# First feed forward: up and down slabs interleaved, 13 slabs by seven block products, two weight sums added by DMA

## The chip, the cores and the metric

The kernel runs on one core of a Trainium2 chip. The metric is the device time of one execution in microseconds (us), the median of several runs. TensorE does the matrix products into PSUM (eight banks of 512 float32 columns for each of 128 partitions), VectorE and ScalarE the elementwise work, Pool (GpSimd) small things and some DMA issues, SP the DMA issues of the weights. Each engine works through a queue of its own, in order; they meet by semaphores.

## The reference

Two transformer blocks on 256 tokens of width 1024, float32. The part that is changed is the feed forward of the first block:

```python
u = rmsnorm(h, norm_ff_g) @ w1          # (256, 1024) @ (1024, 4096)
h = h + jnp.square(jax.nn.relu(u)) @ w2 # (256, 4096) @ (4096, 1024)
```

Before it stand the mixer and a cross attention, behind it the second block (gated mixing of three branches and a convolutional feed forward). All of them stream weights in the same way.

## The kernel before

Weights stream through the core in slabs of 256 rows or columns, 128 x 2048 elements (1 MB) each, in the order that `plan` lists. A slab `n` is loaded by SP into one of three buffers (`raw`, slot `n % RING`), then split: ScalarE rounds it to `whi` (function `hi`, line 1389) and VectorE takes the rest, `wlo = raw - whi` (function `lo`, line 1944). A product in float32 accuracy is three matmuls (function `mm3`, lines 718 to 720): high by high, high by low, low by high. `whi` and `wlo` have three slots too, so slab `n + 3` is split when TensorE is done with slab `n` (`slab_done`), and slab `n + 3` is loaded when slab `n` is split (`lo_ready`). Each engine's program lists these steps by slab: at step `n`, ScalarE and VectorE do what comes after slab `n` and then split slab `n + 3`.

The feed forward has 16 up slabs (`w1`, called u0 to u15 here) and 16 down slabs (`w2`). An up slab gives 256 hidden columns in transposed form: `t_slab`, 16 products of 128 x 128 by 128 x 256, into one of three banks of `tb` in turn. ScalarE takes relu out of the bank into `ru` (line 1695), which frees it (`act_emptied`); VectorE squares into `sq` (line 2305), ScalarE copies the high part (`hid_hi`, line 1699), VectorE the low part (`hid_lo`, line 2319). All 16 up slabs come first, then the 16 down slabs, each adding its 256 hidden rows to four banks of `acc` (`row_slab`, 8 products of 128 x 128 by 128 x 512, for two tiles of tokens, two halves of columns and two blocks of rows).

Six of the down slabs (1, 3, 5, 7, 9, 11; list `SEVEN`) are done with seven products in place of eight, by Strassen's scheme in Winograd's form (`seven_slab`). A slab is four blocks B11, B12, B21, B22. Three products use blocks of the slab itself, four use sums of blocks (forms). VectorE makes four weight sums in place in `raw` (`forms`, lines 2331 to 2335), ScalarE copies their high parts (`forms_hi`, line 1717, into the room of `xhi`) and VectorE the low parts (`forms_lo`, line 2343). On the hidden side VectorE makes sums of the four 128-column blocks after the square (lines 2310 to 2313), with high and low parts in `sum_hi` and `sum_lo`. Four of the seven products collect in four banks of `tb` over the six slabs and are added to `h` by VectorE after slab 11 (`fold`, lines 2351 to 2361); the other three go straight into `acc`.

The last down slab (`last_row_slab`) goes by quarters: after each quarter VectorE adds it to `h` (`residual`, line 1984), and TensorE transposes the sum for the next stage (`turn`).

Of the kernel before, what the change touches and what calls it, by code (L numbers as in the profile page):

```python
# [16 lines left out]
F32 = mybir.dt.float32  # L17
# [7 lines left out]
P = 128  # L25
D = 1024
KT = D // P
T = 256
# [7 lines left out]
RING = 3  # L36
SLAB = 2048
# [6 lines left out]
PAD = 16  # L44


def plan(w):
# [40 lines left out]
    cols("w1", w["w1"], 0, 16)  # L88
    rows("w2", w["w2"], 16)
# [20 lines left out]
def two_blocks(nc, w, out):  # L110
# [14 lines left out]
    SEVEN = [first["w2"] + j for j in (1, 3, 5, 7, 9, 11)]  # L125

    landed = [0] * NS
    for n in range(NS):
        landed[n] = (landed[n - RING] if n >= RING else 0) + (16 if n < first["cv"] and n not in SEVEN else 32)

    with ExitStack() as ctx:
# [63 lines left out]
        with ExitStack() as r3:  # L195
            hid_hi = sb("hid_hi", [P, FF1 // P, T], F32R, at=r3)
            hid_lo = sb("hid_lo", [P, FF1 // P, T], F32R, at=r3)
            ru = sb("ru", [P, 512], at=r3)
            sq = sb("sq", [P, 512], at=r3)
            sum_hi = sb("sum_hi", [P, len(SEVEN), 3 * P], F32R, at=r3)  # L200
            sum_lo = sb("sum_lo", [P, len(SEVEN), 3 * P], F32R, at=r3)
# [55 lines left out]
        memT_in, mem2T_in, ml = sem("memT_in"), sem("mem2T_in"), sems("ml", "hi lo")  # L257
# [25 lines left out]
        sev = sems("sev", "t hi lo kept folded")  # L283
# [31 lines left out]
        lasts = [first["wo"] + 3, first["xo"] + 3, first["w2"] + 15, first["w3"] + 3, NS - 1]  # L315
# [3 lines left out]
        TURNED = {"h1": first["wo"] + 3, "h2": first["xo"] + 3, "x2": first["w2"] + 15}  # L319
# [116 lines left out]

        FORMS_HI, FORMS_LO = (room[:, 32:32 + SLAB].rearrange("p (s c) -> p s c", c=512) for room in (xhi_room, xlo_room))
        sums = xn[:, 0, 0:3 * P]

        def halves(t):  # L440

            return t[:, 0:4:3, :], t[:, 1:3, :]
# [11 lines left out]
        def _(sp):  # L454
            def load(n, src=None, wait=None):
# [59 lines left out]
            for n in range(RING + 1, first["w1"]):  # L515
# [5 lines left out]
            w1v = w["w1"].rearrange("(k p) c -> p k c", p=P)  # L521
            loop("w1", lambda i, u: w1v[:, :, bass.ds(i * 768 + u * 256, 256)], 5)
            load(first["w1"] + 15)
            for n in range(first["w2"], first["cv"]):
                load(n)
# [7 lines left out]
        def _(pool):  # L533
# [115 lines left out]
            pool.dma_start(turned_mem, w["mem2T"]).then_inc(mem2T_in, 16)  # L649
# [4 lines left out]
            for m in range(1, LEVELS):  # L654
# [8 lines left out]
            scale_cross()  # L663
            square_scale()
# [50 lines left out]
        def _(pe):  # L715
# [17 lines left out]
            def t_slab(n, hi, lo, bank, value=None, fresh=None):  # L733
# [4 lines left out]
                for c in range(slabs[n][3] // P):  # L738
                    o = tb[:, bank + c // 2, (c % 2) * T:(c % 2) * T + T]
# [35 lines left out]
            def seven_slab(j, hi, lo):  # L775

                n = first["w2"] + j
                i, k = SEVEN.index(n), 2 * j
                b_hi, b_lo = slab(whi, n, 2).rearrange("p k (s c) -> p (k s) c", c=512), \
                    low_slab(n, 2).rearrange("p k (s c) -> p (k s) c", c=512)  # L780
                first_one, last_one = i == 0, i == len(SEVEN) - 1

                def whole(kt, t):
                    return hi[:, kt, t * P:t * P + P], lo[:, kt, t * P:t * P + P]

                def summed(a):
                    return sum_hi[:, i, a * P:a * P + P], sum_lo[:, i, a * P:a * P + P]

                split_ready(n)
                mm3(tb[:, 0, :], *whole(k, 0), b_hi[:, 1, :], b_lo[:, 1, :], first_one, last_one)  # L790
                mm3(acc[:, 0, 0, :], *whole(k + 1, 0), b_hi[:, 2, :], b_lo[:, 2, :], False, False)
                mm3(acc[:, 1, 0, :], *summed(2), b_hi[:, 3, :], b_lo[:, 3, :], False, False)
                pe.wait_ge(sev["lo"], 2 * i + 1)
                mm3(tb[:, 1, :], *summed(0), FORMS_HI[:, 0, :], FORMS_LO[:, 0, :], first_one, last_one)
                mm3(tb[:, 3, :], *whole(k, 1), FORMS_HI[:, 3, :], FORMS_LO[:, 3, :], first_one, last_one)
                pe.wait_ge(sev["lo"], 2 * i + 2)
                mm3(tb[:, 2, :], *summed(1), FORMS_HI[:, 1, :], FORMS_LO[:, 1, :], first_one, last_one)
                mm3(acc[:, 0, 1, :], *whole(k + 1, 1), FORMS_HI[:, 2, :], FORMS_LO[:, 2, :], False, False)\
                    .then_inc(slab_done, 1)
# [396 lines left out]
            n0 = first["w1"] + 1  # L1196
            with pe.Fori(0, 5) as i:
                for u in range(RING):
                    pe.wait_ge(act_emptied, i * RING + (act_evacs[n0 + u] - RING))
                    t_slab(n0 + u, XHI["h2"], XLO["h2"], (u + 1) % RING, i * RING + (n0 + u + 1))  # L1200

            for j in range(15):
                pe.wait_ge(ffn["lo"], j + 1)
                if j == 1:
                    emptied(first["w1"] + 15)
                if first["w2"] + j in SEVEN:
# [1499 lines left out]
```

## Time and profile before

| | us |
|---|---|
| median of 3 runs | 884.2 (884.06 to 884.23) |
| the profiled execution | 884.08 |
| its span, first to last instruction | 882.2 |
| TensorE busy | 874.6 (99%) |
| VectorE busy | 647.6 (73%) |
| ScalarE busy | 502.4 (57%) |
| Pool busy | 117.9 (13%) |
| moved by DMA | 160.67 MB, 182 GB/s over the span |

The span is what the rows of the trace cover; the rest of an execution's time (1.9 us) lies around it. A row of a matmul gives its length in a pipeline, so consecutive matmuls overlap in the rows; the pace of a slab is read from the starts. "Idle before" tells how long an engine had stood still before an instruction and which other instruction released it.

### The profile page before, as it was taken

The numbers are of one execution on the slowest core, as the hardware profiler recorded it, in microseconds if no ns is written. First come the engines' busy times: TensorE is split into PE (matmuls) and PEld (weight loads), VectorE is DVE, ScalarE is ACT, GpSimd is POOL, SyncE is SP. The second block draws the span as 40 slices with busy tenths as digits, with TensorE's granted clock in tenths as the row PEclk, the third lists the DMA queues.
The fourth block names the chain that finished last, engine by engine and source line by source line (L and its number), as shares of the span: only waits on it lengthen the run. The fifth ranks groups of instructions, "written<-read, shape, count | busy, mean of one in ns | idle before, by whom it ended". The sixth has DMA issues, their size and how long they took to land.

```text
span 882.2 us, 15673 instructions
## 1 busy us (share of the span) xinstructions
PE 874.6 (99%) x6269; PEld 809.7 (92%) x6269; DVE 647.6 (73%) x881; ACT 502.4 (57%) x741; POOL 117.9 (13%) x136
## 2 busy tenths in 40 slices
PE   9999999999999999999999999999999999999997
PEld 9998988989989999888899989999998899999886
DVE  5887987656538887998775548978686788888643
ACT  7786655546547555545473356656634766666432
POOL 5561433000001000000142250001000100000000
PEclk9999999999999999999999999999999999999999
DMA  9969444354535666466556554354556386676641
GB/s 304 319 226 311 164 144 144 104 177 148 172 94 187 195 195 197 160 230 219 191 184 210 191 191 141 104 188 138 174 191 191 105 225 195 194 198 201 192 143 48
DMA packets 137399, 160.67 MB, mean 182 GB/s; under 512 B 4161, under 2 KB 113857, under 8 KB 137089
## 3 DMA queue, kind: packets, MB, share of 16 engines
q1 hardware_dynamic: 135280, 152.83, 54.1%
q0 software_dynamic: 1344, 6.03, 2.0%
q10 hardware_dynamic: 720, 1.06, 0.3%
q8 instruction: 38, 0.62, 0.3%
q14 instruction: 17, 0.13, 0.1%
HBM read 158.86 MB, written 1.05 MB: 181 GB/s over the span
## 4 chain that ended last, share of the span: by engine, by line
PE 98%; issue 1%; ACT 0%; DVE 0%; POOL 0%; DVEq 0%; POOLq 0%; ACTq 0%
PE tb L718 18%; PE tb L719 18%; PE tb L720 18%; PE acc L718 11%; PE acc L720 11%; PE acc L719 11%; PE acc L1043 1%; PE tb L1242 0%; PE tb L1122 0%; PE acc L1272 0%; PE tb L1140 0%; PE acc L1140 0%; PE acc L1290 0%; PE acc L1122 0%; PE tb L1241 0%
## 5 line engine op out<-in xcount | busy, mean ns | idle before, releaser
L1944 DVE TENSOR_TENSOR wlo<-raw,whi 128x2048 fp32r<-128x2048 f32 (+1 forms) x138 | 313.9, 2279 | 118.5 <-ACT whi L1389 117.9
L1389 ACT ACTIVATE whi<-raw 128x2048 fp32r<-128x2048 f32 (+1 forms) x138 | 261.4, 1896 | 140.6 <-PE acc L720 85.2
L718 PE MATMUL tb<-xhi,whi 128*128 128x256 f32 x1192 | 331.8, 278 | 0.2
L719 PE MATMUL tb<-xlo,whi 128*128 128x256 f32 x1192 | 329.5, 276 | 0.0
L720 PE MATMUL tb<-xhi,wlo 128*128 128x256 f32 x1192 | 329.5, 276 | 0.0
L718 PEld LDWEIGHTS tb<-xhi,whi 128*128 128x128 f32 x1192 | 224.1, 188 | 1.1 <-issue 1.0
L719 PEld LDWEIGHTS tb<-xlo,whi 128*128 128x128 f32 x1192 | 224.2, 188 | 0.1
L720 PEld LDWEIGHTS tb<-xhi,wlo 128*128 128x128 f32 x1192 | 224.0, 188 | 0.0
L720 PE MATMUL acc<-whi,xlo 128*128 128x512 f32 x112 | 44.0, 393 | 0.0
L718 PE MATMUL acc<-whi,xhi 128*128 128x512 f32 x112 | 43.8, 392 | 0.0
L719 PE MATMUL acc<-wlo,xhi 128*128 128x512 f32 x112 | 43.8, 391 | 0.0
L1893 ACT ACTIVATE cy<-tb,cols 128x256 f32<-128x256 f32 x44 | 22.5, 561 | 32.3 <-PE tb L720 32.3
L711 POOL TENSOR_TENSOR rs<-rs,half_neg 128x1 f32<-128x1 f32 x6 | 3.3, 553 | 266.8 <-DVE rs L2563 266.8
L719 PE MATMUL acc<-wlo,vhi 128*128 128x512 f32 x88 | 34.2, 389 | 0.0
L718 PE MATMUL acc<-whi,vhi 128*128 128x512 f32 x88 | 34.2, 389 | 0.0
L720 PE MATMUL acc<-whi,vlo 128*128 128x512 f32 x88 | 34.2, 389 | 0.0
L718 PE MATMUL acc<-whi,hid_hi 128*128 128x512 f32 x86 | 33.6, 391 | 0.0
L720 PE MATMUL acc<-whi,hid_lo 128*128 128x512 f32 x86 | 33.5, 389 | 0.0
L719 PE MATMUL acc<-wlo,hid_hi 128*128 128x512 f32 x86 | 33.5, 389 | 0.0
L2619 DVE SCALAR_TENSOR_TENSOR cy<-tb,cols,cy 128x255 f32<-128x255 f32 x44 | 19.2, 478 | 14.1 <-ACT cy L1893 14.1
L718 PE MATMUL tb<-mhi,whi 128*128 128x256 f32 x96 | 27.1, 282 | 0.0
L720 PE MATMUL tb<-mhi,wlo 128*128 128x256 f32 x96 | 26.6, 277 | 0.0
(448 smaller groups left out, 1598.2 us busy)
## 6 DMA issues: line engine op xcount, KB each, us to landing
raw<-in_w_in SPq DMA_DIRECT2D x37, 1024.0 KB, 5.2
raw<-in_w SPq DMA_DIRECT2D x26, 1024.0 KB, 5.4
raw<-in_w_up SPq DMA_DIRECT2D x44, 512.0 KB, 5.0
raw<-in_w_down SPq DMA_DIRECT2D x22, 512.0 KB, 4.2
raw<-in_w_xkv SPq DMA_DIRECT2D x8, 1024.0 KB, 5.3
raw<-in_w_out SPq DMA_DIRECT2D x8, 1024.0 KB, 4.9
raw<-in_w SPq DMA_DIRECT2D x12, 512.0 KB, 4.5
raw<-in_w_mem_kv SPq DMA_DIRECT2D x4, 1024.0 KB, 5.2
```

Of the source, the lines that this page charges most:

```text
L711: pool.tensor_tensor(r, r, half_neg[:, 0:1], ALU.pow).then_inc(tail_rs, 1)
L718: pe.matmul(o, a_hi, b_hi, start=start, stop=False)
L719: pe.matmul(o, a_hi, b_lo, start=False, stop=False)
L720: return pe.matmul(o, a_lo, b_hi, start=False, stop=stop)
L1043: last = pe.matmul(acc[:, 1, t, i * 64:i * 64 + 64], a[:, s], lvl_view(b[:, s], m)[:, :, 1, :], start=True, stop=True)
L1389: act.activation(whi[:, n % RING, cut], raw[:, n % RING, cut], ACT.Copy).then_inc(hi_ready, 1)
L1893: last = act.activation(cy[:, b, g, :], tb[:, b, g * T:g * T + T], ACT.Identity, scale=cols[:, bass.ds(j + a, 1)], bias=cols[:, bass.ds(j ...
L1944: dve.tensor_tensor(low(n)[:, cut], raw[:, n % RING, cut], whi[:, n % RING, cut].bitcast(F32), ALU.subtract).then_inc(lo_ready, 1)
L2619: last = dve.scalar_tensor_tensor(cy[:, b, g, 1:], tb[:, b, g * T:g * T + T - 1], cols[:, bass.ds(j + c, 1)], cy[:, b, g, 1:], ALU.mult, A ...
```

## The change

The up and down slabs of the first feed forward are no longer done in two runs but interleaved, in the order of `FIRST_FFN` (u an up slab, s a down slab by seven products, n a plain one). 13 of the 16 down slabs go by seven products; 3, 7 and 11 stay plain. A down slab needs the hidden rows of its own up slab only.

- PSUM: the seven products use four banks of `tb` and three of `acc`. The eighth bank, `acc[:, 1, 1, :]`, takes all up slabs but u0. TensorE starts an up slab when ScalarE has done relu and square of the one before.
- Weight sums: the scheme's signs are set so that T1 = B11 + B12, T3 = B12 + B22, T2 = T1 + B22, T4 = T2 + B21. SP loads B12 and B22 into a new tile `pairs` (two buffers) beside B11, B21 and B22 in `raw`; then Pool issues a DMA that adds B11 and B12 to them on the way (`add_blocks`). VectorE makes T2 and T4 (`weight_sums`). The forms have rooms of their own with two buffers (`forms_hi`, `forms_lo`).
- Hidden side: ScalarE squares too; VectorE makes four sums of 128 columns (`hidden_sums`); the seven blocks are split together (896 columns).
- The fold comes after s15, with n7 and n11 behind it, from a copy of the four `tb` banks that ScalarE makes in `pairs`.
- TensorE's loop over w1 and SP's are unrolled. Two semaphores of the transposed memories become one.

```diff
+FIRST_FFN = "u0 u1 u2 s0 u3 s1 u4 s2 u5 u6 s4 u7 s5 u8 s6 u9 u10 s8 u11 s9 u12 s10 u13 u14 s12 u15 s13 n3 s14 s15 n7 n11"
...
                 if n in SEVEN:
                     forms = raw_forms(n)
-                    for c, slots in enumerate((slice(1, 3), slice(0, 4, 3))):
-                        sp.dma_start(forms[:, slots, :], ap[:, :, c * 512:c * 512 + 512]).then_inc(raw_landed[n % RING], 16)
+                    i = SEVEN.index(n)
+                    sp.dma_start(forms[:, 1:3, :], ap[:, :, 0:512]).then_inc(raw_landed[n % RING], 16)
+                    sp.dma_start(forms[:, 3, :], ap[:, 1, 512:1024]).then_inc(raw_landed[n % RING], 16)
+                    if i >= 2:
+                        sp.wait_ge(sev["lo"], 2 * i - 3)
+                    sp.dma_start(pairs[:, i % 2, :, :], ap[:, :, 512:1024]).then_inc(raw_landed[n % RING], 16)
...
+            def add_blocks(n):
+
+                i = SEVEN.index(n)
+                pool.wait_ge(raw_landed[n % RING], landed[n])
+                if i >= 2:
+                    pool.wait_ge(sev["lo"], 2 * i - 3)
+                pool.dma_start(pairs[:, i % 2, :, :], slabs[n][1][:, 0, :].rearrange("p (a c) -> p a c", a=2),
+                               accum_op=ALU.add).then_inc(sev[f"acc{i % 2}"], 16)
+
+            add_blocks(SEVEN[0])
             square_scale()
 
             pool.dma_start(xn[:, 1, :], w["final_norm_g"].rearrange("(a c) -> a c", a=1).broadcast_to([P, D])
                            ).then_inc(gfin_in, 16)
+            for n in SEVEN[1:]:
+                add_blocks(n)
             gain_fin()
...
-            n0 = first["w1"] + 1
-            with pe.Fori(0, 5) as i:
-                for u in range(RING):
-                    pe.wait_ge(act_emptied, i * RING + (act_evacs[n0 + u] - RING))
-                    t_slab(n0 + u, XHI["h2"], XLO["h2"], (u + 1) % RING, i * RING + (n0 + u + 1))
-
-            for j in range(15):
+            for kind, j in ORDER[1:-1]:
+                if kind == "u":
+                    emptied(UP[j - 1] if j > 1 else first["xo"] + 3)
+                    t_slab(UP[j], XHI["h2"], XLO["h2"], None, whole=acc[:, 1, 1, :])
+                    continue
                 pe.wait_ge(ffn["lo"], j + 1)
...
-            pe.wait_ge(sev["folded"], 1)
-            last_row_slab("x2", hid_hi, hid_lo, 30)
+            j = PLAIN[-1]
+            pe.wait_ge(sev["kept"], 1)
+            last_row_slab("x2", plain_hidden(hid_hi, j), plain_hidden(hid_lo, j), 0)
...
+            def relu_square(j):
+
+                act.wait_ge(slab_done, UP[j] + 1)
+                if j:
+                    act.wait_ge(act_emptied, act_evacs[UP[j - 1]])
+                    act.activation(ru[:, :], acc[:, 1, 1, :], ACT.Relu).then_inc(act_link, 1)
...
+                act.wait_ge(act_link, count[0])
+                act.wait_ge(ffn["lo"], j)
+                act.activation(sq[:, 0:512], ru[:, :], ACT.Square).then_inc(act_emptied, 1)
...
+            for n, (kind, j) in enumerate(ORDER[:-1], first["w1"]):
+                if kind == "u":
+                    relu_square(j)
+                hi(n + RING)
+                if kind == "u":
+                    hidden_hi(j)
+                if n + RING in SEVEN:
+                    form_hi(n + RING, 0)
+                    form_hi(n + RING, 1)
+                if n == SEVEN[-1]:
+                    act.wait_ge(slab_done, n + 1)
+                    act.activation(pairs[:, :, :, :].rearrange("p i s c -> p (i s) c"), tb[:, :, :], ACT.Copy)\
+                        .then_inc(sev["kept"], 1)
...
+            def hidden_sums(j):
+
+                a11, a21, a12, a22, s1, s2, s4 = (sq[:, s * P:s * P + P] for s in range(7))
+                dve.wait_ge(act_emptied, act_evacs[UP[j]])
+                link(dve.tensor_tensor(s1, a22, a21, ALU.subtract))
+                dve.tensor_tensor(a21, a11, a21, ALU.subtract)
+                link(dve.tensor_tensor(s2, s1, a11, ALU.add))
+                dve.tensor_tensor(s4, a12, s2, ALU.subtract).then_inc(ffn["sq"], 1)
...
+            def weight_sums(n):
+
                 i = SEVEN.index(n)
...
+                dve.wait_ge(sev[f"acc{i % 2}"], 16 * (i // 2) + 16)
+                dve.wait_ge(lo_ready, n + 1)
+                link(dve.tensor_tensor(t2, t1, b22, ALU.add))
+                dve.tensor_tensor(b21, t2, b21, ALU.add).then_inc(sev["t"], 1)
...
+            for n, (kind, j) in enumerate(ORDER[:-2], first["w1"]):
+                if kind == "u" and seven(j):
+                    hidden_sums(j)
+                lo(n + RING)
+                if kind == "u":
+                    hidden_lo(j)
+                if n + RING in SEVEN:
+                    weight_sums(n + RING)
+                    form_lo(n + RING, 0)
+                    form_lo(n + RING, 1)
+                if n == SEVEN[-1]:
+                    fold()
```

`load` keeps its rule that the buffer of a seven-product slab is reloaded only when both of its forms are split (`if n - RING in SEVEN: sp.wait_ge(sev["lo"], ...)`). `form_hi` waits for the addition (first half) and for `weight_sums` (second half); `form_lo` follows it on VectorE.

## Rows read from the trace of the kernel before

**Rows 1.** The page's chain that ended last: shares of the span by engine.

```profile
PE 98%; issue 1%; ACT 0%; DVE 0%; POOL 0%; DVEq 0%; POOLq 0%; ACTq 0%
```

**Rows 2.** Busy us by stage, PEclk (granted clock), DMA share, GB/s.

```profile
272.00:446.00 174.00, 174.00 (x1170) 159.52 (x1169) 145.12 (x162) 99.77 (x110) 7.57 (x9) 1.00 0.60 196
```

**Rows 3.** Timeline of TensorE: start us, length us, line: first matmuls of slabs.

```profile
274.99 0.29 PE L718 MATMUL tb<-xhi,whi 128*128 128x256 f32 x1
...
356.66 0.39 PE L718 MATMUL acc<-whi,hid_hi 128*128 128x512 f32 x1
...
413.11 0.39 PE L718 MATMUL tb<-whi,hid_hi 128*128 128x512 f32 x1
...
417.87 0.39 PE L718 MATMUL acc<-whi,hid_hi 128*128 128x512 f32 x1
```

**Rows 4.** Waits from 270 to 446 us: total us, times, longest us.

```profile
ACT xhi L1717 <- DVE raw L2332: 17.6, 5, 4.0
```

**Rows 5.** Groups by line and shape, 272 to 441: busy us, mean ns, idle before.

```profile
L1944 DVE TENSOR_TENSOR wlo<-raw,whi 128x2048 fp32r<-128x2048 f32 x26 | 59.3, 2289 | 13.6 <-ACT whi L1389 13.5
L1389 ACT ACTIVATE whi<-raw 128x2048 fp32r<-128x2048 f32 x26 | 49.6, 1909 | 11.3 <-PE acc L720 11.3
...
L2343 DVE TENSOR_TENSOR xlo<-raw,xhi 128x1024 fp32r<-128x1024 f32 x12 | 14.5, 1221 | 0.0
L1717 ACT ACTIVATE xhi<-raw 128x1024 fp32r<-128x1024 f32 x12 | 12.7, 1062 | 19.6 <-DVE raw L2332 17.6 <-DVE raw L2335 2.0
...
L1944 DVE TENSOR_TENSOR wlo<-raw,whi 128x1536 fp32r<-128x1536 f32 x6 | 10.5, 1757 | 1.3 <-ACT whi L1389 1.2
...
L1695 ACT ACTIVATE ru<-tb 128x512 f32<-128x512 f32 x15 | 9.0, 601 | 30.9 <-PE tb L720 30.9
L1389 ACT ACTIVATE whi<-raw 128x1536 fp32r<-128x1536 f32 x6 | 8.9, 1488 | 3.8 <-PE acc L720 3.8
...
L2331 DVE TENSOR_TENSOR raw<-raw 128x512 f32<-128x512 f32 x6 | 4.2, 692 | 0.2
...
L2310 DVE TENSOR_TENSOR xn<-sq 128x128 f32<-128x128 f32 x6 | 1.8, 292 | 0.2
```

**Rows 6.** Timelines of ScalarE and of VectorE at the end of u0.

```profile
276.97 0.38 ACT L1707 ACTIVATE ru<-acc 128x256 f32<-128x256 f32 x1
...
277.38 0.69 DVE L2305 TENSOR_TENSOR sq<-ru 128x512 f32<-128x512 f32 x1 [0.40 <-ACT ru L1707]
```

**Rows 7.** DMA issues: count, KB each, us to landing; last: Pool's five into `xn`.

```profile
raw<-in_w SPq DMA_DIRECT2D x26, 1024.0 KB, 5.4
...
raw<-in_w SPq DMA_DIRECT2D x12, 512.0 KB, 4.5
...
gpost<-in_norm_ffn_post POOLq DMA_DIRECT2D x1, 512.0 KB, 4.0
...
DMA to landing us min/median/max: 5.4/7.0/7.8
```

**Rows 8.** Timeline of VectorE: first and last operation of the fold.

```profile
418.77 0.75 DVE L2351 SCALAR_TENSOR_TENSOR h<-ru,rs,h 128x512 f32<-128x512 f32 x1 [1.16 <-ACT ru L1731]
...
423.79 0.75 DVE L2351 SCALAR_TENSOR_TENSOR h<-ru,rs,h 128x512 f32<-128x512 f32 x1
```

**Rows 9.** TensorE's timeline at start and end; last: a stretch as in rows 2.

```profile
1.26 2.19 PE L906 MATMUL tb<-negF 128*128 128x128 f32 x9 [1.26 <-DVE negF L2008]
...
7.06 0.41 PE L720 MATMUL tb<-xhi,wlo 128*128 128x256 f32 x1
7.27 0.41 PE L718 MATMUL tb<-xhi,whi 128*128 128x256 f32 x1
...
7.84 0.28 PE L718 MATMUL acc<-xhi,whi 128*128 128x256 f32 x1
...
876.26 0.39 PE L720 MATMUL acc<-whi,vlo 128*128 128x512 f32 x1
...
881.50:882.20 0.70, 0.00 (x0) 0.00 (x0) 0.00 (x0) 0.00 (x0) 0.00 (x0) 0.53 0.00 0
```

More of the change, by code:

```diff
@@ L44, with ffn_order @@
 PAD = 16
+def ffn_order():
+    return [(step[0], int(step[1:])) for step in FIRST_FFN.split()]
 def plan(w):
@@ L87, in plan @@
     rows("xo", w["w_xo"], 4)
-    cols("w1", w["w1"], 0, 16)
-    rows("w2", w["w2"], 16)
+    first["w1"] = len(slabs)
+    for kind, j in ffn_order():
+        if kind == "u":
+            slabs.append(("T", w["w1"][:, j * 256:(j + 1) * 256].rearrange("(k p) c -> p k c", p=P), 8, 256, "act"))
+        else:
+            ap = w["w2"][j * 256:(j + 1) * 256, :].rearrange("(k p) c -> p k c", p=P)
+            slabs.append(("N", ap, 2, 1024, "dve" if len(slabs) == first["w1"] + 31 else None))
     wi = w["w_in_2"]
@@ L796, in seven_slab, with plain_slab @@
                 pe.wait_ge(sev["lo"], 2 * i + 2)
-                mm3(tb[:, 2, :], *summed(1), FORMS_HI[:, 1, :], FORMS_LO[:, 1, :], first_one, last_one)
-                mm3(acc[:, 0, 1, :], *whole(k + 1, 1), FORMS_HI[:, 2, :], FORMS_LO[:, 2, :], False, False)\
-                    .then_inc(slab_done, 1)
+                mm3(tb[:, 2, :], *part(S2), *form(T2), first_one, last_one)
+                mm3(acc[:, 0, 1, :], *part(A22), *form(T4), first_one, False).then_inc(slab_done, 1)
+            def plain_slab(j):
+                n, hi, lo = DOWN[j], plain_hidden(hid_hi, j), plain_hidden(hid_lo, j)
+                split_ready(n)
+                b_hi, b_lo = slab(whi, n, 2), low_slab(n, 2)
+                for t in range(TT):
+                    for c in range(2):
+                        for k in range(2):
+                            a, w = slice(t * P, t * P + P), slice(c * 512, c * 512 + 512)
+                            last = mm3(acc[:, c, t, :], hi[:, k, a], lo[:, k, a], b_hi[:, k, w], b_lo[:, k, w],
+                                       t * c == 1 and k == 0 and j == PLAIN[0], False)
+                last.then_inc(slab_done, 1)
@@ L1689, in _ @@
             sumsq("h2", h)
-            def relu_step(bank, done, j, dst):
-                act.wait_ge(slab_done, done)
-                act.activation(ru[:, :], tb[:, bank, :], ACT.Relu).then_inc(act_emptied, 1)
-            def relu_hi(j):
-                act.wait_ge(ffn["sq"], j + 1)
-                last = act.activation(hid_hi[:, 2 * j:2 * j + 2, :], sq[:, :], ACT.Copy)
-                if first["w2"] + j in SEVEN:
-                    last = act.activation(sum_hi[:, SEVEN.index(first["w2"] + j), :], sums, ACT.Copy)
-                last.then_inc(ffn["hi"], 1)
@@ new lines, in hidden_hi, with form_hi @@
+            def hidden_hi(j):
+                if seven(j):
+                    act.wait_ge(ffn["sq"], sum(seven(i) for i in range(j + 1)))
+                else:
+                    act.wait_ge(act_emptied, act_evacs[UP[j]])
+                cut = hidden_place(j)
+                act.activation(hid_hi[:, cut], sq[:, 0:cut.stop - cut.start], ACT.Copy).then_inc(ffn["hi"], 1)
+            def form_hi(n, half):
+                i = SEVEN.index(n)
+                if i >= 2:
+                    act.wait_ge(slab_done, SEVEN[i - 2] + 1)
+                if half == 0:
+                    act.wait_ge(sev[f"acc{i % 2}"], 16 * (i // 2) + 16)
+                else:
+                    act.wait_ge(sev["t"], i + 1)
+                src, cut = form_places(n, half)
+                act.activation(forms_hi[:, i % 2, cut, :], src, ACT.Copy).then_inc(sev["hi"], 1)
```

224 lines of the change are left out of this document (88 added, 136 removed).

## Prediction

> **What bounds the kernel now.** I read the chain that ended last first: 98% of it is TensorE [rows 1]. So time is won or lost here only where TensorE gets less work or waits. Then the table by stage, for the first feed forward [rows 2]: TensorE is busy for all of its 174 us, VectorE for 145 (83%), the DMA engines for 0.60 at 196 GB/s. So nothing is late there, but VectorE has only a sixth of its time to spare. Next the pace of a slab from the timeline. The first w1 slab ends at 274.99 and the first w2 slab starts at 356.66, with 15 w1 slabs between: 81.67 / 15 = 5.44 us each. A seven-product slab runs from 413.11 to 417.87: 4.76 us for 21 matmuls, 0.227 each [rows 3]; a plain one has 24 of them, 5.44. (The 0.39 us of a row is its pipelined length, not its pace.) Last the waits: ScalarE waited 17.6 us in five turns of up to 4.0 for the weight sums of VectorE, before it could copy them into forms [rows 4]. That costs nothing today, since nobody needs what is queued behind that copy soon. It is the row to keep in mind.
>
> **The gain.** Seven more slabs lose 3 of 24 matmuls: 7 x 3 x 0.227 = 4.8 us of TensorE. There is nothing else to win on the path: TensorE has no wait to remove.
>
> **What an up/seven pair costs off the path.** Durations are from [rows 5]; one for 896 columns lies between those for 512 and 1024. VectorE: wlo of an up slab 2.29, wlo of three quarters 1.76, four hidden sums 4 x 0.29, hid_lo 1.09, two weight sums 2 x 0.69, two form_lo 2 x 1.22: 10.1 us. ScalarE: 1.91 + 1.49 + two form copies 2 x 1.06 + relu 0.60 + square 0.60 + hid_hi 0.95 = 7.7. TensorE: 5.44 + 4.76 = 10.2. So in the alternating stretches VectorE is as loaded as TensorE and has no slack; the slabs that are split ahead cover it. The sums given to the DMA (2 x 0.69 for each seven slab) are what brings VectorE down to this. Unrolling the loop of w1 I cost at nothing: slabs outside loops have the same pace [rows 3]. The merged semaphore of the two transposed memories waits for the same transfers, so nothing there either; nor for Pool's steps that move behind the additions (the scale of h2, final_norm_g), which are first used at the fold and after it.
>
> **The new wait: one bank for all up slabs.** Before, u slabs went round three banks of tb. Now each but the first goes to the same half of acc, and TensorE may start one only when ScalarE has done relu and square of the one before. Where a seven slab stands between, its 4.76 us cover this. In four places two up slabs are neighbours (u1 u2, u5 u6, u9 u10, u13 u14) and nothing covers it. With ScalarE free it would be relu 0.60 + square 0.60 + hand-overs of some 0.5 = 1.7. (A hand-over is 0.03 at 277.35 to 277.38 [rows 6]; I estimate up to 0.1 each with the drain of a matmul, 0.39 long.) But ScalarE isn't free: its queue is in order, and ahead of that relu stand the two form copies for the slab three places on, the second of which waits for VectorE's weight sums, as in [rows 4], and now for a DMA as well.
>
> *u2.* Relu of u0 ends at 277.35 as now [rows 6]. Square and hand-over: 278.1. Four hidden sums to 279.4, beside ScalarE's copy of s0 (1.49) to 279.6. On VectorE wlo 1.76, hid_lo 1.09, two weight sums 1.4: 283.9. ScalarE: second form copy 1.06, relu and square of u1: 286.2. u1 ends at 274.99 + 5.44 = 280.4. TensorE waits 5.7 us.
>
> *u6, u10, u14* have the same neighbourhood. Let X be the end of u3 on TensorE (u7, u11). VectorE works on the forms of s2 then: relu, square 1.6, copy 1.5, wlo 1.76, hid_lo 0.69, sums 1.4, two form_lo 2.5: done at X + 9.6 with hand-overs. Only then may SP load s4, three places on, since `load` waits for both forms of the slab that held the buffer. The load is 1,280 KB in three DMAs; 512 KB took 4.5 and 1024 KB 5.4 [rows 7], so some 5.9. Then Pool issues the accumulating DMA, which lands after L. Then two sums 1.4, the form copy 1.06, relu and square of u5 1.2, hand-overs 0.5. Together X + 19.7 + L. TensorE ends u5 at X + 4.76 + 5.44 + 4.76 + 5.44 = X + 20.4. The wait is L - 0.7, and not under some 3: that is what copy, wlo, sums and form copy take after s2 has ended, if the addition is early.
>
> **L: no accumulating DMA is in the trace.** The nearest rows are Pool's plain ones: 4.0 for 512 KB in a quiet stretch, and 5.4 to 7.8 with a median of 7.0 for transfers of mostly 1024 KB [rows 7]. The addition brings 512 KB and reads as much of its target, so I take 7.0; low end 4.0, since it can't be quicker than the same transfer without an addition; high end 11, two such transfers in turn (7.0 + 4.0). The load on the DMA supports the upper half: a pair moves 1.05 + 1.31 + 0.52 = 2.88 MB in 10.2 us, 283 GB/s, against 196 at a share of 0.60 now [rows 2], which is a share of 0.87 before the price of adding. The wait is then 6.3 each, 18.9 for three (9.9 to 30.9). The Trainium skill (DMA: Bandwidth & Descriptors, Anatomy of one DMA) would give a plain Pool DMA of 512 KB some 3.2 us, an estimate from its fit of 2.0 us plus the bytes at 436 GB/s; the sum would then stand at the floor of 3 us for each wait. The rows of 4.0 and more say that it is longer here.
>
> **The end of the stage.** The fold's eight operations now follow s15, with two slabs behind them in place of four. In the trace they run from 418.77 to 424.54, 5.8 us [rows 8]. After the end of s15, at E: ScalarE splits a slab (1.9) and copies four banks (about 1.9), VectorE does wlo until E + 4.5, the fold until E + 10.3, and the first residual (0.75, as the fold's last row) until E + 11.1. TensorE has n7 (5.44) and two quarters of n11 (2.7) and needs the residual at E + 8.2. It waits 3.0 us (0 if VectorE gets to the fold 3 us earlier, 5 if ScalarE is late with the bank copy). For s15 and n7, whose splits come late behind the last addition, 0.5 (0 to 4).
>
> **The clock.** TensorE's last matmul starts at 876.26; the granted clock is 0.53 from 881.5 on, the half level (1.2 GHz) [rows 9]. At the start it works from 1.26, and at 7.06 matmuls of 256 columns are still 0.21 apart, twice the 0.113 of a w1 slab (5.44 / 48); the one at 7.84 has the length of a w1 row again (0.28, and 0.29 at 274.99). So four waits of 5.7 to 6.3 us can each drop the clock, and getting it back costs up to 6.5 us at half pace, 3.2 lost. I take 1.6 for each, 6.4 in all (0 to 13). The Trainium skill (TensorE: Matmul & The Clock Gate, HAM oscillation) says that a wait which lets the clock fall makes the next group of matmuls start slow, every time anew. By that rule the forecast holds; without it case B does.
>
> **Sum**, from the profiled execution: span 882.2 and 1.9 around it, 884.1, which is the median (884.2) within 0.1. -4.8 + 5.7 + 18.9 + 3.0 + 0.5 + 6.4 = +29.7: 913.8 us.
>
> **The rivals.**
> A (forecast): waits at the four neighbours as above, clock lost: 914, some 907 to 922. Chance 0.40.
> B: the same waits, the clock held: 884.1 + 23.3 = 907. For it: the half level shows only behind an idle stretch about as long as these waits [rows 9]. 0.25.
> C: the addition is quick (L = 4.0). Waits of 3.3, and the clock holds: -4.8 + 5.7 + 9.9 + 3.0 = +13.8, 898. For it: the 4.0 row; against it: the DMA's load. 0.13.
> D: the addition is slow and the DMA engines become the bound (L = 11): 30.9 in the three waits, 4 at s15 and n7: -4.8 + 5.7 + 30.9 + 3.0 + 4 + 6.4 = +45, 929. For it: a share of 0.87 before adding. 0.15.
> E (not slower): the bank is freed a slab earlier than I read. `emptied` compares with a running count of ScalarE's slabs; if that runs one ahead, a whole slab covers ScalarE's lateness, no u slab waits, and -4.8 + 3.0 gives 882.3. It decides from waits of under 1.8 us in all. Against it: one count is raised for each slab, and two writers of one bank need the wait. 0.07.
>
> **Numbers.** Runs of before lie within 0.2 us, and some 0.2% (1.8 us) can be told from no change. Range 897 to 930: it leaves out E, and what of D lies above and of C below. Faster 0.04, same 0.03 (both E), slower 0.93.
>
> **What would show it.** TensorE idle before the first matmul of u2, u6, u10 and u14, released by ScalarE's square, some 6 us each, and before the first turn behind n11, released by VectorE (3 us); no gap at other slabs. ScalarE idle before form copies, released by VectorE, and VectorE idle before its first weight sum of s4, s8, s12, for the DMA. Matmuls 0.45 us apart for some us after such a gap (A) or not (B). A landing of the additions near 4, 7 or 11 us tells C, A and D apart. Wrong would be: even gaps at all seven slabs (the DMA as a bound), or none at the up neighbours.

## The result and the profile after

The changed kernel takes 927.9 us (median of 4 runs, 925.98 to 929.01) against 884.1 beside it: a ratio of 1.0492 (1.0474 to 1.0511). It is 43.7 us slower. The forecast was 914 with a range of 897 to 930, so the time lies in the range, near its upper end. The profiled execution has a span of 926.1 us, 43.9 more than before; the accounts below are made from spans.

First the chain that ended last, shares of the span by engine (before: [rows 1]):

```profile
PE 79%; issue 8%; DMA 5%; DVE 5%; ACT 3%; POOL 0%; SPq 0%; POOLq 0%; DVEq 0%; ACTq 0%
```

A fifth of the chain is no longer TensorE. Next the stage's own stretch (busy us with counts of PE, PEld, DVE, ACT and POOL, then PEclk, DMA share, GB/s), which answers to [rows 2]:

```profile
272.00:490.00 218.00, 179.92 (x1152) 164.47 (x1152) 157.91 (x185) 122.67 (x135) 17.47 (x21) 0.91 0.69 201
```

TensorE stands for 38 of 218 us and its granted clock is 0.91 on average. No other engine is full: VectorE has 72%, the DMA engines 0.69. So something waits for something in turn, and the list of TensorE's waits (total us, times, longest) says where:

```profile
PE acc L763 <- ACT sq L1762: 34.2, 4, 9.8
PE tb L916 <- DVE h L2049: 3.8, 1, 3.8
PE acc L763 <- ACT pairs L1796: 0.2, 1, 0.2
```

Four waits for ScalarE's square and one for VectorE's residual. On TensorE's timeline they stand ahead of u2, u6, u10, u14 and the first turn, the five places of the prediction and, but for 0.2 us ahead of n7, no other. The second row of u6 belongs to the clock: it is 0.41 us long, where such a row has 0.28 at full pace:

```profile
286.21 0.58 PE L763 MATMUL acc<-xhi,whi 128*128 128x256 f32 x1 [5.25 <-ACT sq L1762]
...
334.51 0.58 PE L763 MATMUL acc<-xhi,whi 128*128 128x256 f32 x1 [9.50 <-ACT sq L1762]
334.89 0.41 PE L764 MATMUL acc<-xlo,whi 128*128 128x256 f32 x1
...
382.70 0.58 PE L763 MATMUL acc<-xhi,whi 128*128 128x256 f32 x1 [9.64 <-ACT sq L1762]
...
430.82 0.58 PE L763 MATMUL acc<-xhi,whi 128*128 128x256 f32 x1 [9.77 <-ACT sq L1762]
...
480.74 0.44 PE L916 MATMUL tb<-ident,h 128*128 128x128 f32 x2 [3.76 <-DVE h L2049]
```

What stands ahead of u6 is told by four timelines. X, the end of u3 and the start of s1, is at 304.35. SP:

```profile
313.53 0.37 SPq L498 DMA_DIRECT2D raw<-in_w  x1
313.94 1.21 SPq L499 DMA_DIRECT2D raw<-in_w  x1
315.19 0.44 SPq L502 DMA_DIRECT2D pairs<-in_w  x1
316.36 0.37 SPq L506 DMA_DIRECT2D raw<-in_w  x1
320.22 0.37 SPq L498 DMA_DIRECT2D raw<-in_w  x1
...
321.14 0.47 SPq L502 DMA_DIRECT2D pairs<-in_w  x1
```

Pool:

```profile
321.52 0.86 POOL L703 DMA_DIRECT2D pairs<-in_w  x1 [22.58 <-DMA pairs<-in_w]
```

VectorE:

```profile
330.74 0.69 DVE L2392 TENSOR_TENSOR raw<-pairs,raw 128x512 f32<-128x512 f32 x1 [6.12 <-DMA pairs<-in_w]
```

ScalarE:

```profile
330.80 1.06 ACT L1783 ACTIVATE forms_hi<-pairs 128x1024 fp32r<-128x1024 f32 x1 [8.04 <-DMA pairs<-in_w]
332.25 1.06 ACT L1783 ACTIVATE forms_hi<-raw 128x1024 fp32r<-128x1024 f32 x1 [0.40 <-DVE raw L2393]
333.21 0.58 ACT L1755 ACTIVATE ru<-acc 128x512 f32<-128x512 f32 x1
333.82 0.63 ACT L1762 ACTIVATE sq<-ru 128x512 f32<-128x512 f32 x1
```

SP issues the load of s4 at X + 9.2. It lands 8.0 us later (Pool's issue at 321.52 shows it), the addition another 9.2 us later, and form copies, relu and square take 3.8 to u6. TensorE had finished u5 at 324.84. From then to 333.21 the relu of u5, 1.2 us with the square, stood behind two copies for another slab. Beside the load of s4 SP issued that of u7 (316.36), and the three DMAs for s5 (320.22 to 321.14) just ahead of the addition. The 13 additions, from issue to landing:

```profile
DMA to landing us min/median/max: 5.4/5.7/9.2
```

Those of s4, s8 and s12 are the longest (9.2, 8.8 and 9.0); the one at 344.75, with no load just ahead, took 5.5. The DMA engines are 0.69 busy over the stage, but 0.89 during the addition of s4 (columns as above):

```profile
321.52:330.74 9.22, 3.49 (x31) 3.29 (x30) 1.76 (x2) 1.23 (x1) 0.86 (x1) 0.89 0.89 255
```

ScalarE's two kinds of wait before form copies answer to [rows 4], where VectorE's sums were the only one:

```profile
ACT forms_hi L1783 <- DMA pairs<-in_w: 26.7, 4, 8.0
...
ACT forms_hi L1783 <- DVE raw L2393: 23.8, 13, 2.5
```

Three long ones for additions and one of 3.1 us at s15, and 13 short ones for VectorE. Last the clock, in the wait for u6, in its first 4.5 us and after them (columns as above):

```profile
330.00:334.50 4.50, 0.00 (x0) 0.00 (x0) 3.68 (x5) 3.27 (x5) 0.86 (x1) 0.50 0.41 56
334.50:339.00 4.50, 4.49 (x21) 4.49 (x22) 3.77 (x7) 2.59 (x2) 0.00 (x0) 0.51 1.02 284
339.00:342.20 3.20, 3.20 (x30) 3.20 (x30) 0.58 (x1) 0.00 (x0) 0.00 (x0) 1.00 0.76 252
```

TensorE came out of the wait at the half level (1.2 GHz) and worked there for 4.5 us, then at the full one. The 48 matmuls of u2, u6, u10 and u14 took 7.9, 7.65, 7.45 and 7.3 us in place of 5.44.

The account of spans: -4.8 (seven products; a slab of them still takes 4.77, an up slab 5.47) + 34.2 (four waits) + 8.5 (slow matmuls, 2.46 + 2.21 + 2.01 + 1.86) + 3.8 + 0.2 = 41.9. Of the 2.0 us that are left, part is that idle time is counted from the end of a pipelined row and not from its pace; the rest I haven't assigned.

### The profile page after: what moved, and what is told of

Its sections match the earlier page's. It is cut to its first block, busy times and chain, and to the rows that moved or that the text cites. A ratio compares the mean times of both kernels' runs of the same rounds, so it can differ in the third digit from the quotient of the medians.

```text
span 926.1 us, 15681 instructions
## 1 busy us (share of the span) xinstructions
PE 880.2 (95%) x6248; PEld 814.3 (88%) x6248; DVE 659.2 (71%) x903; ACT 524.7 (57%) x765; POOL 123.5 (13%) x149
## 4 chain that ended last, share of the span: by engine, by line
PE 79%; issue 8%; DMA 5%; DVE 5%; ACT 3%; POOL 0%; SPq 0%; POOLq 0%; DVEq 0%; ACTq 0%
PE tb L763 14%; PE tb L765 14%; PE tb L764 14%; PE acc L763 10%; PE acc L765 9%; PE acc L764 9%; DMA pairs<-in_w 4%; PE acc L1103 1%; ACT whi L1447 1%; DVE wlo L2009 1%; DVE raw L2392 1%; DVE raw L2393 1%; DVE forms_lo L2400 1%; DVE hid_lo L2381 1%; DMA raw<-in_w_in 1%
## 5 line engine op out<-in xcount | busy, mean ns | idle before, releaser
L763 PE MATMUL tb<-xhi,whi 128*128 128x256 f32 x952 | 265.6, 279 | 0.3 <-issue 0.2
L764 PE MATMUL tb<-xlo,whi 128*128 128x256 f32 x952 | 263.2, 276 | 0.0
L765 PE MATMUL tb<-xhi,wlo 128*128 128x256 f32 x952 | 263.2, 276 | 0.0
L763 PEld LDWEIGHTS tb<-xhi,whi 128*128 128x128 f32 x952 | 179.0, 188 | 1.4 <-issue 1.2
L763 PE MATMUL acc<-xhi,whi 128*128 128x256 f32 x304 | 88.8, 292 | 34.2 <-ACT sq L1762 34.2
L763 PEld LDWEIGHTS acc<-xhi,whi 128*128 128x128 f32 x304 | 60.9, 200 | 35.3 <-ACT sq L1762 34.9
L764 PE MATMUL acc<-xlo,whi 128*128 128x256 f32 x304 | 87.7, 288 | 0.0
L765 PE MATMUL acc<-xhi,wlo 128*128 128x256 f32 x304 | 87.4, 288 | 0.0
L764 PEld LDWEIGHTS acc<-xlo,whi 128*128 128x128 f32 x304 | 61.0, 201 | 0.4
L765 PEld LDWEIGHTS acc<-xhi,wlo 128*128 128x128 f32 x304 | 60.7, 200 | 0.0
L763 PE MATMUL acc<-whi,xhi 128*128 128x512 f32 x112 | 43.9, 392 | 0.0
L764 PE MATMUL acc<-wlo,vhi 128*128 128x512 f32 x88 | 34.2, 389 | 0.0
L763 PE MATMUL acc<-whi,vhi 128*128 128x512 f32 x88 | 34.2, 389 | 0.0
```

Source lines behind the costliest of these rows:

```text
L763: pe.matmul(o, a_hi, b_hi, start=start, stop=False)
L764: pe.matmul(o, a_hi, b_lo, start=False, stop=False)
L765: return pe.matmul(o, a_lo, b_hi, start=False, stop=stop)
```

## The experiments

Theory Q is the prediction's: up slabs have one bank, ScalarE's queue is in order, and where two up slabs are neighbours the relu that frees the bank stands behind two form copies, which stand behind the addition. Its rivals: the bank and the copies take that time by themselves; the DMA queues set the pace; VectorE does; the slow matmuls aren't the clock. Each kernel was timed beside the kernel before; "above" means above that. "Slow" is what the 48 matmuls of a slab take over 5.44.

**e1: no addition.**

```diff
-                pool.dma_start(pairs[:, i % 2, :, :], ..., accum_op=ALU.add).then_inc(sev[f"acc{i % 2}"], 16)
+                pool.sem_inc(sev[f"acc{i % 2}"], 16)
```

> Edit: the Pool step that adds the two upper weight blocks in flight issues no DMA; it waits for the same load and then raises the same semaphore at once. T1 and T3, and with them T2 and T4, so lack one block each; everything else is computed. Theory Q (the relu that frees the one up bank stands in ScalarE's queue behind two form copies, which stand behind the addition's landing): the waits ahead of u6, u10 and u14 fall from 9.7 us to 2.8 to 3.8, the slow matmuls behind them (2.0 us each) go with them, u2's wait stays near 5.3 because there the copies and not the addition are late, the turn's wait stays: 14.5 to 17.5 us above the kernel before, 898.6 to 901.6 us. Rival B (the one bank and the copies in themselves are what takes the time, the addition lands beside them): the three waits lose 2 us at most, 920 us or more. Rival D (the queues are full and the loads set the pace; the addition is 10 of 171 MB): 925 us, with the waits on the loads instead.

911.6 us, a ratio of 1.0310 (1.0292 to 1.0328). TensorE's waits:

```profile
PE acc L762 <- ACT sq L1761: 16.6, 4, 5.3
PE tb L915 <- DVE h L2048: 3.3, 1, 3.3
```

u2 5.3 as before; u6, u10 and u14 3.9, 3.3 and 4.1, where Q had 2.8 to 3.8, so the addition is some 6 of each 9.7 us. But I had let the slow matmuls go with waits so short, and they stayed (2.2, 1.5, 3.0, 1.8, and 2.9 behind the turn). They are most of the 10 us by which I was off.

**e2: the relu ahead of the form copies.**

```diff
+                nxt = [ORDER[n + d - first["w1"]] for d in (1, 2) if n + d <= FFN_END]
+                ahead = n + RING in SEVEN and [k for k, _ in nxt] == ["u", "u"]
-                if kind == "u":
+                if kind == "u" and j not in early:
                     relu_square(j)
...
                 if kind == "u":
                     hidden_hi(j)
+                if ahead:
+                    relu_square(nxt[0][1])
+                    early.append(nxt[0][1])
                 if n + RING in SEVEN:
```

> Edit: where two up slabs follow each other, ScalarE does the relu and the square of the first of them ahead of the two form copies of the seven slab to come; nothing else moves and all is computed. Theory Q: the waits ahead of u6, u10 and u14 fall from 9.7 to about 1.8 us (relu, square and three handovers), u2's from 5.3 to about 2.5, none is followed by slow matmuls; but the additions still land as late, VectorE's sums and low parts come as late as before, and the slabs behind wait on VectorE instead (about 3.5 us ahead of u7, u11 and u15, some 1 us at others): about 23 us above the kernel before, 907 us. If VectorE had room to spare, only the turnaround stays: 10 us above, 894 us. Rival D (loads set the pace): 925 us or more, with the waits moved ahead of s4, s8 and s12.

910.9 us, 1.0314 (1.0283 to 1.0346), 4 us above what Q gave. The timeline has 2.31 us ahead of u2, 1.35 ahead of u6, u10 and u14, and 3.21, 2.40 and 2.21 ahead of u7, u11 and u15. Nothing but ScalarE's order was changed, and more than 8 us of each 9.7 are gone: it is the order that turns a late addition into this wait. Q had no slow matmuls; u2, u7 and u11 have them (1.6, 1.8 and 1.7 us), which is more than the 4 us. The waits behind are VectorE's, which still stands for the addition before it gets to the hidden sums of u5:

```profile
327.66 0.69 DVE L2399 TENSOR_TENSOR raw<-pairs,raw 128x512 f32<-128x512 f32 x1 [5.63 <-DMA pairs<-in_w]
```

**e3 and e5: the loads beside s4, s8 and s12 held back.** e3 holds the next load until the blocks of s4 are there and the one behind it until the addition is; e5 holds both until the addition is.

```diff
 # e3, in load(n); LONE holds s4, s8 and s12
+                for m in LONE:
+                    if n == m + 1:
+                        sp.wait_ge(raw_landed[m % RING], landed[m])
+                    elif n == m + 2:
+                        i = SEVEN.index(m)
+                        sp.wait_ge(sev[f"acc{i % 2}"], 16 * (i // 2) + 16)
 # e5, in load(n)
+                for m in LONE:
+                    if n == m + 1:
+                        i = SEVEN.index(m)
+                        sp.wait_ge(sev[f"acc{i % 2}"], 16 * (i // 2) + 16)
```

> Edit: SyncE issues the load of the slab after s4, s8 and s12 only when their own blocks have landed, and the load after that only when their addition has landed; nothing else moves and all is computed. Theory Q with the late landings put down to transfers issued beside them: the load of s4 lands 6 us after its issue instead of 7.9, the addition 5.5 us instead of 9.2, the waits ahead of u6, u10 and u14 fall from 9.7 to about 5, with half of the slow matmuls behind them: about 28 us above the kernel before, 912 us. Rival L (the addition takes 9 us there for another reason, its own two halves or the read of what it adds to): landings and waits stay, 928 us. Rival D (the queues are full): holding two loads back moves all that follows, above 930 us.

> Edit: the load of the slab after s4, s8 and s12 is issued only when the addition of that slab has landed (in e3 it went out just ahead of the addition, 320.4 and 320.6 us, so the addition still had 1 MB beside it); nothing else moves and all is computed. Theory Q with the late landing put down to the transfer beside it: the addition lands 5.4 to 5.7 us after its issue, as the ones without a load just ahead do, the waits ahead of u6, u10 and u14 are about 5 us instead of 9.7 (and 7.2 to 8.3 in e3), the clock still falls in them: 913 us. Rival L (the addition takes 8 to 9 us there whatever lies beside it): landings of 8 us and more, waits of 7 us or more, 921 us or more.

e3: 925.4 us, 1.0474 (1.0456 to 1.0491), not to be told from the changed kernel and 13 us above what Q gave. The edit put u7's 1 MB where s5's load had been, just ahead of the addition:

```profile
320.37 0.37 SPq L513 DMA_DIRECT2D raw<-in_w  x1
```

```profile
320.59 0.86 POOL L710 DMA_DIRECT2D pairs<-in_w  x1 [21.47 <-DMA pairs<-in_w]
```

Those are SP's and Pool's timelines; the landing of that one addition:

```profile
DMA to landing us min/median/max: 8.0/8.0/8.0
```

Those of s8 and s12 took 8.0 and 8.5. The waits were 7.2, 8.3 and 7.4 us. e5 has nothing beside the addition: 917.3 us, 1.0379 (1.0358 to 1.0400). The same addition:

```profile
DMA to landing us min/median/max: 5.5/5.5/5.5
```

The waits fell to 5.1, 5.1 and 4.6, as Q had them. So the long landing of these three comes from the load issued just ahead of them, and with none the DMA engines are 0.61 busy in place of 0.89:

```profile
321.23:326.73 5.50, 4.20 (x38) 4.00 (x36) 2.14 (x2) 1.23 (x1) 0.86 (x1) 1.00 0.61 95
```

The time fell 4 us less than expected, since slow matmuls stayed in full (2.8, 2.9, 1.6) and 1.7 more came behind the turn.

**e4: the waits filled.**

```diff
+                    if j in (6, 10, 14):
+                        pe.wait_ge(warm_ready, 2)
+                        for _ in range(82):
+                            pe.matmul(tb[:, 3, 0:T], negF[:, 0:P], XHI["h2"][:, 0, :], start=False, stop=False)
                     emptied(UP[j - 1] if j > 1 else first["xo"] + 3)
...
+            dve.memset(negF[:, :].bitcast(U32), 0).then_inc(warm_ready, 1)
```

> Edit: ahead of u6, u10 and u14 TensorE does 82 matmuls of 256 columns with a weight block of zeros into a bank that sums up (9.3 us at 0.113), then waits as before; the sums are unchanged by them. Theory K (the 2.0 us that each of these slabs takes above 5.44 are the clock, fallen in the wait): u6, u10 and u14 take 5.45 to 5.5 us instead of 7.3 to 7.65, the granted clock of the stretches 330:350, 370:390 and 430:450 is 0.95 or more, 6.0 us less than the changed kernel, 921.8 us. Rival (the slow start is the operands or the bank, not the clock): no less than 927 us, and matmuls of 0.21 us stay behind the wait.

919.8 us, 1.0410 (1.0388 to 1.0431): 8.1 less than the changed kernel with 246 matmuls more. The filled wait with the start of u6, and the rest of u6 with the first of s4 (columns as in the windows above):

```profile
324.00:334.50 10.50, 10.50 (x94) 10.41 (x93) 4.75 (x8) 4.68 (x5) 0.86 (x1) 1.00 0.79 178
334.50:339.00 4.50, 4.50 (x41) 4.46 (x40) 3.29 (x2) 1.35 (x3) 0.00 (x0) 1.00 0.83 268
```

The clock holds: TensorE does 41 matmuls in 4.5 us where it did 21, and u6, u10 and u14 take 5.4 to 5.5 us. So the slow matmuls are the clock; at the three slabs they had cost 6.1 us. Most of the other 2 us are fillings shorter than the waits (some 1.5 in all) and a quicker u2 (0.6).

**e6: e1 and e2 together.**

> Edits of e1 and e2 together (relu and square ahead of the form copies, and no addition issued, so that T1 to T4 lack a block each). In e2 the waits ahead of u7, u11 and u15 (3.2, 2.4, 2.2 us) are left. Theory Q (they too are the landing of the addition, for which VectorE's stream stands, with the hidden sums behind it): they go; left are 2.3 us ahead of u2, 1.4 us each ahead of u6, u10 and u14, 3.3 us ahead of the turn and the clock behind the first and the last of these: 8.6 us above the kernel before in the span, 892 us. Rival V (they are VectorE's own work, some 10.1 us of each pair's 10.24): waits of 2 us and more stay ahead of u7, u11 and u15, 900 us or more.

893.8 us, 1.0111 (1.0094 to 1.0128).

```profile
PE acc L762 <- ACT sq L1763: 6.4, 4, 2.3
PE tb L915 <- DVE h L2055: 3.8, 1, 3.8
```

The waits of e2 ahead of u7, u11 and u15 are gone, so they were the addition's too, reached through VectorE. Addition and order together explain 34 of the 44 us. What is left would not go with a free addition: an up slab behind another on one bank waits 1.35 us for relu, square and handovers.

**e7: VectorE makes the two sums.**

```diff
+                link(dve.tensor_tensor(pairs[:, i % 2, 1, :], pairs[:, i % 2, 1, :], pairs[:, i % 2, 0, :], ALU.add))
+                dve.tensor_tensor(pairs[:, i % 2, 0, :], pairs[:, i % 2, 0, :], raw_forms(n)[:, 1, :], ALU.add).then_inc(sev["acc0"], 1)
```

> Edit: no addition in flight; VectorE adds the two blocks itself, two more sums of 0.69 us for each seven slab, and ScalarE's form copy waits for these; nothing else moves and all is computed. Theory Q (what stands ahead of the relu decides, whoever makes it): the sums come after VectorE's low part of the same slab, so the copies wait nearly as long: 7 us ahead of u2 (5.3 before), 7 to 8 us ahead of u6, u10 and u14, 2 us more in the last slabs, and the clock behind each wait: 925 us. Rival A (only the landing of a transfer is the trouble, and VectorE has room): waits of 4 us as in e1, 911 us.

924.1 us, 1.0462 (1.0444 to 1.0479). Without any addition in flight:

```profile
PE acc L760 <- ACT sq L1759: 24.2, 4, 6.7
```

6.7 ahead of u2, 5.3 to 6.2 at the other three, where Q had 7 to 8, and 2.6 in the last slabs. So giving the sums to the DMA is not the mistake; what stands ahead of the relu is.

**e8: e2 and e5 together.**

> Edits of e2 and e5 together (relu and square ahead of the form copies, loads held until the addition has landed), all is computed. Theory Q: u2 waits 2.3 us, u6, u10 and u14 1.4 us each, VectorE is late by 1 to 1.5 us at some slabs behind them, the turn waits 3.8 us: 14 to 17 us above the kernel before, 899 us. Rival V (VectorE's work bounds the stage once the relu is free): no better than e2, 908 us or more.

915.5 us, 1.0350 (1.0326 to 1.0373), 5 us worse than e2. My forecast was 16 us off, and the rival's number came out, but not for its reason alone: ScalarE waits for additions at ten slabs (six in e2). I put that down to each load held back, which delays the next slab's addition.

```profile
ACT forms_hi L1790 <- DMA pairs<-in_w: 27.6, 10, 5.9
```

**e10: e2, and the addition's target loaded a slab earlier.**

```diff
                     sp.dma_start(dst, src).then_inc(raw_landed[n % RING], 16)
+                    load_pairs(n + 1)
...
-                pool.wait_ge(raw_landed[n % RING], landed[n])
...
+                pool.wait_ge((lam_in, bias_in)[i % 2], (64, 16)[i % 2] + 16 * (i // 2) + 16)
```

`load_pairs` loads B12 and B22 of the next slab, if that is a seven slab, on a semaphore of their own, for which alone Pool now waits.

> Edits of e2 (relu and square ahead of the form copies) and another: the blocks that the addition adds to are loaded one slab earlier, right behind the load before, so that the addition is issued and lands before the slab's other blocks; the order of the stage is that of the changed kernel, all is computed. Theory Q (once the addition lands before it is wanted it costs no more than none): the waits of e6 (2.3, 1.4 three times, 3.8 ahead of the turn), 893 to 896 us. Rival D (the additions' 7 MB slow the loads beside them wherever they stand): waits on slabs' loads, 903 us or more.

895.7 us, 1.0127 (1.0110 to 1.0144), with all additions made: 32 us less than the changed kernel and 1.9 above e6, which made none. An addition that lands before it is wanted costs next to nothing, whatever it does to the DMA engines.

**e9, e11: no up neighbours on one bank.** e9 leaves n0, n1 and n2 plain, so that u0 to u5 come first, in banks that are still idle, and up and seven slabs alternate from there. e11 adds the early addition of e10.

```diff
+FIRST_FFN = "u0 u1 u2 u3 u4 u5 s3 u6 s4 u7 s5 u8 s6 ... u14 s12 u15 s13 n0 s14 s15 n1 n2"
...
+            return {1: tb[:, 1, :], 2: tb[:, 2, :], 3: tb[:, 3, :], 4: acc[:, 0, 0, :]}.get(j, acc[:, 1, 1, :])
```

> Edit: the order of the stage. The three plain slabs become n0, n1 and n2 instead of n3, n7 and n11, so that the up slabs with no seven slab between them (u0 to u5) all stand at the beginning, where the seven accumulators are not yet in use: u1 to u4 go to four of those banks, u5 and all later ones to the one up bank as before, and from there on up and seven slabs alternate; the same 13 seven slabs and 13 additions, all is computed. Theory Q (what costs is two up slabs on one bank with form copies ahead of the relu, not the additions as such and not the seven products): no wait ahead of any up slab above 1.5 us, 3.8 us ahead of the turn with some 1.5 us of clock behind it, VectorE late by up to 0.3 us in each of ten pairs, 4.8 us gained by the seven products: 0.5 to 4.5 us above the kernel before, 884.5 to 888.5 us. Rival V (VectorE needs as much as TensorE in a pair and falls behind with no pause in 10 pairs): waits that grow from pair to pair, 895 us or more. Rival A (the additions cost wherever they stand): 900 us or more.

> Edits of e9 and the earlier addition of e10 together; all is computed. Theory Q: the additions are not late where up and seven slabs alternate, so landing them earlier changes nothing: within 1 us of e9. Rival A (the additions cost wherever they stand): 5 us or more less than e9. Rival D (they slow the loads): more than 1 us slower than e9.

e9: 904.3 us, 1.0226 (1.0209 to 1.0243). I was wrong by 16 us: the neighbours are gone, but now TensorE waits in the alternating stretch, for low parts of forms and weights that are late behind additions:

```profile
PE tb L766 <- DVE forms_lo L2408: 8.1, 6, 2.1
PE acc L766 <- DVE wlo L2017: 6.4, 6, 1.2
...
ACT forms_hi L1791 <- DMA pairs<-in_w: 27.3, 8, 5.4
```

In the changed kernel no addition was late there; the long waits at the neighbours had let all other queues catch up, and I had read their slack as belonging to the order. e11: 891.3 us, 1.0087 (1.0070 to 1.0104), 12.9 less than e9, where Q had no more than 1: rival A came out, by which the additions cost here too (e9's time fitted V as well). ScalarE waits once for an addition. What is left is 3.8 at the turn, 2.5 elsewhere, and pairs of 10.47 us (4.93 + 5.55) in place of 10.24.

**e12: the best version.** e11 with 12 seven slabs and four plain ones, so that three plain slabs follow s15, and with ScalarE's copy of the banks and VectorE's fold ahead of the next splits (also five idle banks for the first up slabs in place of four, and room for three hidden blocks in place of four):

```diff
-                hi(n + RING)
+                if n != SEVEN[-1]:
+                    hi(n + RING)
...
                         .then_inc(sev["kept"], 1)
+                    hi(n + RING)
...
-                lo(n + RING)
+                if n != SEVEN[-1]:
+                    lo(n + RING)
...
                     fold()
+                    lo(n + RING)
```

> Edits of e11 with three more: 12 seven slabs and four plain ones (n0 to n3) instead of 13 and three, so that three plain slabs stand behind s15; u1 to u5 go to idle accumulators ahead of s4; and at s15 ScalarE's copy of the four banks and VectorE's fold stand ahead of the next slab's high and low parts. All is computed. In e11 the span stands 7.1 us above the kernel before: 4.8 less for the seven products, 2.3 for ten pairs of 10.47 instead of 10.24 us (VectorE), some 3 at the first seven slabs and ahead of n1, 3.8 ahead of the turn and 1.7 of clock behind it. Theory Q: with the fold one slab earlier the wait ahead of the turn and the clock behind it go (5.5 us), one seven slab less gives back 0.7, the rest stays: 1 to 3 us above the kernel before, 885 to 887 us, and no wait over 1.5 us anywhere in the stage. Rival F (the fold is late for another reason than its place behind the low parts): a wait of 2 us or more ahead of the turn stays, 888 us or more. Rival V (VectorE's work sets the end): waits that the fold's going ahead pushes on to n3 or the next stage's first slab, 889 us or more.

886.1 us, 1.0024 (1.0015 to 1.0033): 41.7 us below the changed kernel, and still 2 above the kernel before. All of TensorE's waits in the stage:

```profile
PE acc L770 <- DVE wlo L2023: 1.6, 2, 1.2
PE acc L770 <- ACT sq L1774: 0.8, 1, 0.8
PE tb L770 <- issue: 0.2, 1, 0.2
```

The turn's wait is gone; whether by the third slab behind s15 or by the fold's earlier place this doesn't tell, since both were changed. One period of VectorE in the alternating stretch, with ScalarE's and the start of a TensorE up slab, shows why no gain is left:

```profile
354.13 2.29 DVE L2023 TENSOR_TENSOR wlo<-raw,whi 128x2048 fp32r<-128x2048 f32 x1 [0.58 <-ACT whi L1459]
356.57 0.36 PE L770 MATMUL acc<-xhi,whi 128*128 128x256 f32 x1
...
361.69 1.06 ACT L1795 ACTIVATE forms_hi<-raw 128x1024 fp32r<-128x1024 f32 x1 [2.28 <-DVE raw L2407]
362.66 1.90 ACT L1459 ACTIVATE whi<-raw 128x2048 fp32r<-128x2048 f32 x1
364.59 2.29 DVE L2023 TENSOR_TENSOR wlo<-raw,whi 128x2048 fp32r<-128x2048 f32 x1 [0.58 <-ACT whi L1459]
```

10.46 us from one to the next, with 0.58 idle in it: 9.9 us of work and one wait for ScalarE, against 10.24 us of TensorE. The wait is the old one in small: ScalarE's high part stands behind a form copy, which waits for VectorE's sum, so the two engines go round in a loop of 10.46 us, and TensorE starts its up slab at 356.57, just behind the low part that ends at 356.42. Another order of these copies wasn't tried. Six more seven slabs than before save 4.1 us (6 x 0.68); nine pairs at 0.23 give back 2.1 and the waits 2.6, which makes +0.6; the other 1.9 of the span's +2.5 I haven't assigned. No variant here beats the kernel before.

## Why the prediction was right, and where it was off

- **Place and mechanism of the waits: right.** The four up neighbours and the first turn, each with the releaser that was named, none at other slabs. e2 shows the order of ScalarE's queue as the cause, e1 and e6 the addition ahead of it.
- **u2: right.** 5.3 in the row (5.4 from the pace of u1) for 5.7. It doesn't depend on the addition (e1: 5.3).
- **u6, u10, u14: the term that was mis-sized**, 28.9 for 18.9. From X to u6 it was 9.2 + 8.0 + 9.2 + 3.8 where I had 9.6 + 5.9 + 7.0 + 4.2. Both transfers took 2.1 to 2.2 us more. I took the load's 5.9 from rows of one DMA each; three in turn take 6.9 us even with the next load held back (e3, 313.73 to Pool's 320.59; 7.3 in e5), and u7's load beside them the rest. I took L from Pool's plain transfers and did not look at what SP's queue issues just ahead. At these slabs L is 5.3 to 5.5 when nothing goes out just ahead (e5) and 8.0 to 9.2 behind a load (the changed kernel, e3). My L of 7.0 is none of the two. The case with the high L (D) gave 929, with the DMA engines as the bound. Over the stage nothing of that is seen (a share of 0.69, no wait on a load in TensorE's list, no gaps at other slabs), but for the length of one addition D's crowding is there: 0.89.
- **Some luck in the range.** Case A by itself had 907 to 922, which 927.9 misses; the range held the time because it was kept wide for D.
- **The clock: right in kind, small in size**, 8.5 for 6.4; case B, with the clock held, is out (e4). The Trainium skill (TensorE: Matmul & The Clock Gate, HAM oscillation) has each such wait followed by a slow start, every time anew; the rows of all four slabs agree, 1.9 to 2.5 us each. The wait of 3.8 us ahead of the turn doesn't: the granted clock is 1.00 behind it (480.60 to 485.00).
- **The turn: 3.8 for 3.0**, s15 and n7 0.2 for 0.5. It went in e12, where the fold stands earlier in the queues and one slab more follows s15; which of the two did it is open.
- **The gain of 4.8: right on TensorE** (4.77 a slab), and the warning that VectorE "has no slack" in a pair too. It costs nothing in the changed kernel, whose waits hide it, and becomes the bound as soon as they are gone, with ScalarE's high part in the loop (e12; the pairs of e11 have the same length).
- Case E fell with the first wait, and C with the landings.

## What to carry to other kernels

Before a step that frees a shared buffer is left at its place in an in-order queue, look at what is queued ahead of it and what that waits for: moving one relu and its square ahead of two copies was worth 17 us (e2), and loading the target of a transfer a slab earlier another 15 (e10). Price a new transfer with the ones that its neighbours in the queues will issue beside it, not by a median of rows. And when a long wait is removed, expect the engines that caught up during it to show their own lateness next: here it was additions first (e9), then the 10.46 us that VectorE and ScalarE need for a pair (e12).

## What the runs showed of the hardware

- An accumulating DMA of 512 KB into SBUF: of the 13 in the changed kernel eight landed in 5.4 to 5.7 us, with no load issued in the 4.8 us ahead of them; one, with a load 4.2 us ahead, in 6.5; and four, with 1 to 1.25 MB of loads less than 2 us ahead, in 7.6 to 9.2. A load just behind can do the same: in e5 the addition at 336.11 took 8.3, with none in the 5.4 us ahead and three 0.25 to 1.2 us after it.
- The clock falls in shorter waits than I had thought. Of the 12 waits of 1.35 us ahead of an up slab (e2, e6, e8, e10) none was followed by slow matmuls (0.11 to 0.16 us over 5.44); of the nine between 1.9 and 2.5 us six were (1.55 to 1.77), and all of 3.2 us and more (1.5 to 3.0). Ahead of the first turn it isn't the same every time: behind a wait of 3.8 us the clock is 1.00 in the changed kernel and in e6, and some 0.7 in e5 and e11. In one wait of e1, 3.9 us long, the granted clock is 0.63 over the 3.9 us behind it:

```profile
328.10:332.00 3.90, 3.87 (x22) 3.88 (x23) 3.17 (x6) 2.61 (x2) 0.00 (x0) 0.63 0.67 205
```
